# Two transformer stages in one kernel: the order of steps in the HGRN2 heads, and the weight low parts in four GpSimd instructions

## The reference, cut to what matters

```python
def hgrn2_mixer(h, w_in, lower_bound, norm_gain, w_o):
    q, f, i, g = jnp.split(h @ w_in, 4, axis=-1)
    q = jax.nn.silu(q)
    forget = lb + (1.0 - lb) * jax.nn.sigmoid(f)      # lb is 0 for the first layer of its kind
    log_f = jnp.log(forget)
    k = -jnp.expm1(log_f)
    # S_t = diag(f_t) S_{t-1} + k_t v_t^T ; o_t = S_t^T q_t, per head
    o = hgrn2_chunk_scan(heads(q), heads(k), heads(i), heads(log_f))
    o = rmsnorm(o, norm_gain) * jax.nn.sigmoid(g)
    return o @ w_o
```

## Time and profile before

| | us |
|---|---|
| median of 3 runs | 2027.22 (2027.17 to 2029.34) |
| the profiled execution | 2029.74 |
| its span | 2027.9 |

### The profile page before, as it was taken

How to read it: one execution, slowest core, us unless ns; L and a number is a source line. 1 busy time by engine, 2 the same in 40 slices (tenths; PEclk the granted TensorE clock), 3 DMA queues, 4 the chain that set the end, 5 groups by cost and what they waited for, 6 DMA issues and landing times.

```text
span 2027.9 us, 25756 instructions
## 1 busy us (share of the span) xinstructions
PE 1883.6 (93%) x8662; PEld 1469.3 (72%) x8662; DVE 1187.5 (59%) x1691; ACT 877.1 (43%) x1385; POOL 770.5 (38%) x402
## 2 busy tenths in 40 slices
PE   7999889999999999989899999998999987999988
PEld 5666568887888777878788887886776656776756
DVE  5667668614753677677577317724575556665561
ACT  6676634312433445544443213323554533554441
POOL 3222134444444555456344443443332213332212
PEclk9999999999999999999899999998999999999999
DMA  4212125433532211112145334422221212221212
GB/s 147 63 53 62 42 83 152 148 94 114 166 114 94 83 53 53 52 52 63 31 132 164 109 103 146 155 94 73 73 64 62 63 42 83 70 66 54 71 42 73
DMA packets 49223, 175.28 MB, mean 86 GB/s; under 512 B 5472, under 2 KB 5600, under 8 KB 49136
## 3 DMA queue, kind: packets, MB, share of 16 engines
q1 hardware_dynamic: 42224, 148.98, 23.7%
q10 hardware_dynamic: 6912, 25.17, 3.9%
HBM read 172.03 MB, written 2.10 MB: 86 GB/s over the span
## 4 chain that ended last, share of the span: by engine, by line
PE 38%; DVE 8%; ACT 4%; issue 4%; POOL 1%; ACTq 0%; DVEq 0%; POOLq 0%
PE ps_g L222 11%; PE ps_g L226 11%; PE ps_g L229 10%; DVE scr L1598 1%; DVE scr L431 1%; PE ps_o L1485 1%; PE ps_s L1424 1%; PE ps_zt L931 1%; DVE sml L1664 1%; PE ps_zt L1471 1%; DVE scr L293 1%; ACT scr L425 0%; POOL w_lo L210 0%; DVE scr L1624 0%; DVE a_lo L1632 0%
## 5 line engine op out<-in xcount | busy, mean ns | idle before, releaser
L210 POOL TENSOR_TENSOR w_lo<-raw,w_hi 128x1024 fp32r<-128x1024 f32 x274 | 670.6, 2448 | 1153.0 <-ACT w_hi L205 1153.0
L222 PE MATMUL ps_g<-h_hi,w_hi 128*128 128x512 f32 x1424 | 419.4, 423 | 40.2 <-DVE scr L1572 11.6
L205 ACT ACTIVATE w_hi<-raw 128x1024 fp32r<-128x1024 f32 x274 | 288.9, 1054 | 382.6 <-PE ps_g L229 376.7
L226 PE MATMUL ps_g<-h_lo,w_hi 128*128 128x512 f32 x1424 | 383.1, 399 | 0.2 <-DVE h_lo L255 0.2
L229 PE MATMUL ps_g<-h_hi,w_lo 128*128 128x512 f32 x1424 | 376.9, 394 | 0.0
L222 PEld LDWEIGHTS ps_g<-h_hi,w_hi 128*128 128x128 f32 x1424 | 259.8, 194 | 127.0 <-issue 63.5
L226 PEld LDWEIGHTS ps_g<-h_lo,w_hi 128*128 128x128 f32 x1424 | 275.0, 193 | 63.5 <-DVE h_lo L255 1.2
L229 PEld LDWEIGHTS ps_g<-h_hi,w_lo 128*128 128x128 f32 x1424 | 272.1, 191 | 58.7
L222 PE MATMUL ps_g<-a_hi,w_hi 128*128 128x512 f32 x768 | 205.2, 403 | 17.8 <-DVE a_lo L1632 7.5
L226 PE MATMUL ps_g<-a_lo,w_hi 128*128 128x512 f32 x768 | 197.2, 393 | 0.0
L229 PE MATMUL ps_g<-a_hi,w_lo 128*128 128x512 f32 x768 | 196.7, 392 | 0.0
(11 more groups left out here) (168 smaller groups left out, 2090.3 us busy)
## 6 DMA issues: line engine op xcount, KB each, us to landing
raw<-weights SPq DMA_DIRECT2D x274, 512.0 KB, 3.5
scr<-ada_weights ACTq DMA_DIRECT2D x48, 512.0 KB, 4.4
x<-x_tiles SPq DMA_DIRECT2D x8, 256.0 KB, 5.5
y<-x SPq DMA_DIRECT2D x8, 256.0 KB, 3.2
lvmask<-level_masks SPq DMA_DIRECT2D x1, 512.0 KB, 8.5
mats<-squares SPq DMA_DIRECT2D x1, 448.0 KB, 6.6
vecs<-vectors SPq DMA_DIRECT2D x1, 95.5 KB, 2.0
wgk<-gate_weights SPq DMA_DIRECT2D x1, 32.0 KB, 8.9
```

The source lines that it names most:

```text
L205: nc.scalar.activation(w_hi[:, t.rep % 2], raw[:, raw_slot(t)], ACT.Copy).then_inc(whi_ready, 1)
L210: nc.gpsimd.tensor_tensor(w_lo[:, t.rep % 2], raw[:, raw_slot(t)], w_hi[:, t.rep % 2].bitcast(F32), ALU.subtract).then_inc(wlo_ready, 1)
L222: nc.tensor.matmul(bank[:], w_hi[:, t.rep % 2, kk], rhs(k)[0], start=(first and n == 0), stop=False)
L226: nc.tensor.matmul(bank[:], w_hi[:, t.rep % 2, kk], rhs(k)[1], start=False, stop=False)
```

## The change

In `split_lo`, the one GpSimd subtraction over a tile (128 x 1024) becomes four over 128 x 256; the last one raises the semaphore. In the HGRN2 step, the gate of a part is taken in one piece on ACT, with its last Exp right behind the minimum; on VectorE the query's product follows at once, the front of part 3 of head `a` moves ahead of the scaled queries of level 1, and the front of part 0 of head `g` moves ahead of the selection of level 0 (`hg_sel_dve(dve, a, 1)`) and of the scaled queries of level 2; the decays between tiles come last, after level 6, on GpSimd, ACT and VectorE. The semaphore counts follow: level l is the (l+1)-th.

```diff
 def split_lo(pool, t):
     pool.wait_ge(whi_ready, t.of(1, 1))
-    nc.gpsimd.tensor_tensor(w_lo[:, t.rep % 2], raw[:, raw_slot(t)], w_hi[:, t.rep % 2].bitcast(F32),
-                            ALU.subtract).then_inc(wlo_ready, 1)
+    for i in range(0, KT, 2):
+        ks = slice(i, i + 2)
+        ins = nc.gpsimd.tensor_tensor(w_lo[:, t.rep % 2, ks], raw[:, raw_slot(t), ks],
+                                      w_hi[:, t.rep % 2, ks].bitcast(F32), ALU.subtract)
+    ins.then_inc(wlo_ready, 1)
...
 def hg_front_act(act, g, part):
...
     act.activation(ls_b, u_b[part % 2], ACT.Abs).then_inc(h_ls.abs_ready, 1)
-    h_ls.act(act, g.map(3, max(part - 1, 0)))
-
-def hg_last_act(act, g, part):
-    par = g.rep % 2
     if part == 0:
+        h_ls.act(act, g.map(3))
         act.wait_ge(hkf_ready, g.of(1, 1))
...
         act.activation(kk[par], kf_b, ACT.Exp).then_inc(hk_ready, 1)
     else:
+        n = g.map(3, part - 1)
         dst, done = (qq[par], hqe_ready) if part == 2 else (sg[par], hsg_ready)
-        act.wait_ge(h_ls.ready, g.of(3, part))
+        h_ls.act(act, n)
+        act.wait_ge(h_ls.ready, n.of(1, 1))
         act.activation(dst, dst, ACT.Exp).then_inc(done, 1)
...
 def hg_act(act, g, a, b):
...
-    if a: hg_last_act(act, a, 3)
     if g: hg_front_act(act, g, 0)
     if b: h_unit.act_rstd(act, b, hot_ready, b.v)
     if a: hg_e_act(act, a, 3)
-    if g: hg_last_act(act, g, 0)
...
-    if a: hg_e_act(act, a, 7)
     if a: hg_e_act(act, a, 4)
     if a: hg_e_act(act, a, 5)
     if g: split_hi(act, t + 4)
     if g: hg_front_act(act, g, 2)
     if a: hg_e_act(act, a, 6)
-    if g: hg_last_act(act, g, 2)
+    if a: hg_e_act(act, a, 7)
...
 def hg_front_dve(dve, g, part, stage=0):
...
     h_ls.dve_min(dve, n, bank, qq[par])
+    dve.wait_ge(hqe_ready, g.of(1, 1))
+    nc.vector.tensor_tensor(qq[par], qq[par], bank, ALU.mult).then_inc(hq_ready, 1)
...
 def hg_dve(dve, g, a, b):
     if a:
         hg_front_dve(dve, a, 3, 0)
         hg_qk_dve(dve, a, 0)
+        hg_front_dve(dve, a, 3, 1)
         hg_qk_dve(dve, a, 1)
     if g: hg_front_dve(dve, g, 0, 0)
+    if a: hg_sel_dve(dve, a, 0)
+    if g: hg_front_dve(dve, g, 0, 1)
     if a:
-        hg_front_dve(dve, a, 3, 1)
-        hg_sel_dve(dve, a, 0)
         hg_sel_dve(dve, a, 1)
         hg_qk_dve(dve, a, 2)
-    if g: hg_front_dve(dve, g, 0, 1)
...
         hg_qk_dve(dve, a, 4)
-        hg_qk_dve(dve, a, 7)
         hg_sel_dve(dve, a, 4)
...
         hg_sel_dve(dve, a, 6)
-    if g: hg_q_dve(dve, g)
-    if a: hg_sel_dve(dve, a, 7)
+        hg_qk_dve(dve, a, 7)
+        hg_sel_dve(dve, a, 7)
...
 def hg_pool(pool, g, a, b):
...
-    for i, l in enumerate([(2, 3, 7), (4, 5), (6,)]):
+    for i, l in enumerate([(2, 3), (4, 5), (6, 7)]):
```

More of the change, by code:

```diff
@@ L898, in build_program @@
         ORDER_HG = [NL - 1] + list(range(NL - 1))
[L899 to L905, removed]
         def hg_level_pe(pe, a, n):
@@ L914, in hg_level_pe @@
             else:
-                pe.wait_ge(hkp_ready, exp_n(a, l))
+                pe.wait_ge(hkp_ready, a.of(8, l + 1))
                 pe.wait_ge(hqk_ready, a.of(7, l + 1))
@@ L937, in part @@
                                         stop=True)
-            pe.wait_ge(hkp_ready, exp_n(a, 7))
+            pe.wait_ge(hkp_ready, a.of(8, 8))
             pe.wait_ge(hqr_ready, a.of(4, 4))
@@ L1008, in hg_e_act @@
                 act.wait_ge(hinter_ready, a.of(2))
-                act.wait_ge(hdk_ready, exp_n(a, 7))
+                act.wait_ge(hdk_ready, a.of(8, 8))
                 act.activation(kl_b[:, 0:SEQ - P], d_b[1][:, 0:SEQ - P], ACT.Exp, scale=-1.0).then_inc(hkp_ready, 1)
@@ L1017, in hg_e_act @@
             act.activation(blocks(e2_b[l % 2], n), d[:, :, n:2 * n], ACT.Exp).then_inc(he_ready, 1)
-            act.wait_ge(hdk_ready, exp_n(a, l))
+            act.wait_ge(hdk_ready, a.of(8, l + 1))
             act.wait_ge(hlev_ready, a.of(NL, l if l >= 2 else 0))
@@ L1023, in hg_front_act @@
         def hg_front_act(act, g, part):
+            t, par = g.map(4, T_HG), g.rep % 2
             act.wait_ge(hu_ready, g.of(4, part + 1))
@@ L1141, in hg_qk_dve @@
                                         ALU.mult).then_inc(hqr_ready, 1)
-                dve.wait_ge(hkp_ready, exp_n(a, 7))
+                dve.wait_ge(hkp_ready, a.of(8, 8))
                 nc.vector.tensor_scalar(kv_b[:, 0:P], kl_b[:, 0:P], eb_b[:, 2 * P - 1:2 * P], None,
@@ L1225, in hg_d_pool @@
             pool.wait_ge(hc_ready, a.of(1, 1))
-            pool.wait_ge(hkp_ready, exp_n(a, PREV_HG[l]) if l >= 2 else a.of(8))
+            pool.wait_ge(hkp_ready, a.of(8, max(l - 1, 0)))
             if l == 7:
```

## The result

The changed kernel takes 2002.5 us at the median (four runs, 1998.5 to 2002.6), the kernel before 2027.9 in the same comparison: ratio 0.9869 with a 95% interval of 0.9852 to 0.9886, so 25 us or 1.3% faster. The forecast was 2015, 12 us faster. The sign held, the time lies in the whole range of 1997 to 2036 but outside the forecast's own range of 2005 to 2022; the gain is twice what was summed.

A forecast was written before the change was run, and what follows sets the result against it. TensorE, busy 93% of the span, bounds the kernel, so only its idle or lower clock can be won. Part 1 (-7) and part 2 (-5) take 2027.2 to 2015 us; own range 2005 to 2022, whole range 1997 to 2036.

The forecast's parts named there:

- the second block's term of part 1: Second block: shorter holds of L1572 (2 us) and L1632 (2.8 us) by low parts, about 5 us won.
- part 1: Low parts in four GpSimd pieces of 128x256 instead of one instruction: -7 us, bounds 0 and -14.
- The clock: TensorE's granted clock, 0.95 in HGRN2: no term in the sum, only in part 1's bound, R1 and R3.
- the output projections: Starts of the two output projections: a low part's hold costs about 1 us each, 2 us won.
- Part 2: Former order of steps in HGRN2: waits per head from 3.5 to 2.8 us, -5 us; bounds -22 and +14.
- the prediction's own sign: HGRN2: part 2 is wrong if the pitch of L1229's successor isn't between 38.5 and 39.5 us a head.
- R1: Rival: HGRN2's chain escapes GpSimd, level 2 only 0.4 us late, half-speed stretches shrink; 1997 us, chance 0.15.
- R3: Rival, slower: HGRN2's wait at level 2 becomes the cost, with lower-clock stretches; 2036 to 2041, say 2038 us, chance 0.20.
- Part 1 in HGRN2: Pieces in HGRN2: no gain summed, as the gain is full only for single VectorE instructions.
- The rule of the conserved sum: A run of two-input VectorE instructions meets the pieces one after another, so the sum of waits stays as before.
- the cover: GpSimd's idle and zero wait of w_lo matmuls hide 0.1 us more per tile; without it, 27 us cost.
- R2: Rival: nothing measurable, 2027 us (2023 to 2031), chance 0.15; includes that four queued pieces hold VectorE as one.

The follow-up runs named there:

- the kernel with the decays in the middle: Kernel before with four pieces, gates in one piece and front ahead of level 2's queries, decays left between levels 3 and 4: 1988.1 us, ratio 0.9805.

## Why the prediction was right or wrong

The step that failed is the second block's term of part 1, which was sized at a third of what it brought; it is 10 of the 13 us that the forecast missed. The clock, which the forecast left at nothing, and the pieces in HGRN2 brought about 3 us each, and of the 2 us forecast for the output projections at most 1 came.

**Part 1 in the second block: right place, a third of the size.** I had -2.4 us a layer from two kinds of wait, about 5 us; with the pieces there alone the kernel is 15 us faster, and its layers lost 7.3 and 8.5 us (7.4 and 8.7 in the changed kernel). Little of it is clock: in the changed kernel the idle of the two layers fell by 6.3 and 5.9 us. I had taken L1572 for the instruction that is held. In sum over both layers it isn't: its form with two SBUF inputs went from 14.6 to 18.5 us, and its median over 16 instructions from 0.69 to 1.22 us: more of them now meet a piece, though a short one. What was held is the minimum ahead of it (L431, now L434), and `a_lo` (L1632, now L1621), as these groups of VectorE over the two layers show, first before, then changed (busy us, mean ns of one, idle before):

```profile
L431 DVE SCALAR_TENSOR_TENSOR scr<-scr 128x512 f32<-128x512 f32 x20 | 27.8, 1391 | 6.5 <-ACT scr L427 6.5
L1632 DVE TENSOR_TENSOR a_lo<-scr,a_hi 128x512 fp32r<-128x512 f32 x16 | 25.3, 1582 | 1.4 <-ACT a_hi L1547 1.4
L1572 DVE SCALAR_TENSOR_TENSOR scr<-scr 128x512 f32<-128x512 f32 x16 | 14.6, 912 | 1.6
```

```profile
L1561 DVE SCALAR_TENSOR_TENSOR scr<-scr 128x512 f32<-128x512 f32 x16 | 18.5, 1158 | 0.0
L1621 DVE TENSOR_TENSOR a_lo<-scr,a_hi 128x512 fp32r<-128x512 f32 x16 | 15.7, 982 | 1.4 <-ACT a_hi L1536 1.4
L434 DVE SCALAR_TENSOR_TENSOR scr<-scr 128x512 f32<-128x512 f32 x20 | 14.4, 721 | 5.9 <-ACT scr L430 5.9
```

Wait by wait, in the first layer: L1617's two of 0.7 us went as predicted (-1.4). The wait at 1458.27 fell from 3.73 to 1.57 us, 2.2 and not 1.0: I took one hold off and found ACT's L427 next, but the minima of the three tiles ahead (at 1435.70, 1442.15 and 1448.59) had been held as well, 1.71, 1.71 and 1.70 us, where they now take 0.74, 0.74 and 0.75. The sum over L1572 fell by 1.7 us (its two other waits grew by 0.4 together), a chain that I hadn't looked at, ACT's L1563 behind VectorE, by 1.4, and small ones by about 1.8. The longest L1572 went from 2.46 to 1.23 us and the longest L1632 from 2.90 to 1.23, near the 1.0 forecast.

**Part 2, its sum of waits: right, its pitch: not.** The idle per head was to fall from 3.5 to 2.8 us, 5 us in all; the idle of the stretch fell by 4.9, and with the order alone the span less the clock's cost is 5 us shorter. The wait at level 2 was taken as 2.3 us and is 1.89; the inter part was taken as 0.5 and is 0.50; the waits of 1.57 and 2.87 us are gone. One make-up was wrong: I let three pieces of a low part stand between VectorE's instructions. Only the last piece touches the front, and the 1.0 us that the scans lose is level 4's subtraction (I called it level 3's). By the prediction's own sign part 2 is wrong all the same: the pitch was to be 38.5 to 39.5 us a head and is 37.7. Idle accounts for 0.7 of the 2.0 us and 17.1 us less at 1.2 GHz over seven heads for 1.2 more; that is the clock.

**The clock: left at nothing in the forecast.** A gain of clock stood only in part 1's bound and in R1, a loss in R3, and the sum of the forecast had neither. In the profiled pair the stretch of HGRN2 has 8.5 us of it, the larger part of its 10.0 us less busy time. Over all executions the estimate above leaves 3 to 4 us of it to the change, and 7 of the 12 us to the order alone. The granted clock of 0.95 in the earlier trace rows was in front of me: 5% of 312 us is 16 us of loss, in the stage in which I moved the waits. In the table of stretches less idle goes with less time at 1.2 GHz, roughly and not in every pair of rows.

**Part 1 in HGRN2: nearly nothing, but not for my reason.** I argued that a run of VectorE instructions meets the pieces one after another, so that nothing is won. In the new order the pieces shorten the stretch by 3.6 us (320.4 to 316.8), 0.9 of it idle, so for the forecast itself zero was close. In the order of before they brought 28.8 us in this stage (331.7 to 302.9), 16.6 of it idle; that profiled execution was 7 us faster than its kernel's median. VectorE's busy time in the stretch fell from 227.6 to 201.4 us there, and from 205.9 to 181.7 in the new order: 24 to 26 us less hold in both. The rule of the conserved sum is refuted as a rule. It looks true at level 2 of the new order only because the low part isn't what is met there. One piece is 0.74 us, so a single instruction is held that long and not 2.4; in the order of before the chains behind level 3 and the decays, as I read it, had slack for the short hold and not for the long one. There the 1.57 us wait is at most 0.3, and what is left is this, at the turn:

```profile
743.85 0.66 PE L405 MATMUL ps_zt<-mats,scr 128*128 128x128 f32 x4 [0.62 <-DVE scr L1101]
```

**The starts of the output projections (-2): 1 us at most.** The one behind HGRN2, with its MLP, takes 403.2 us instead of 402.3; all that stands ahead of HGRN2, with the other one in it, takes 667.7 instead of 668.8.

**A piece: 0.74 us, not 0.63.** Four take 3.0 us where 2.40 did one. The Trainium skill (GPSIMD Engine Reference, section 3.1) gave 3.1 by its cycles and my estimate of the dispatch, closer than my row. By that rule the forecast would have been 3 to 4 us higher, and the result is 13 lower: the cover held in every tile of the changed kernel (TensorE's idle before L232 is 0.0 us), so that the longer low part cost TensorE no wait for `w_lo`. Where it fails is in the kernel with the decays in the middle, 1.70 us a head.

**The rivals.** R2's rule, that queued pieces hold VectorE as one, is refuted by the timeline of the changed kernel: a minimum, which reads two tensors, begins and ends while four pieces run.

```profile
1430.77 3.46 POOL L212 TENSOR_TENSOR w_lo<-raw,w_hi 128x256 fp32r<-128x256 f32 x4 [2.35 <-ACT w_hi L205]
...
1432.01 0.75 DVE L434 SCALAR_TENSOR_TENSOR scr<-scr 128x512 f32<-128x512 f32 x1
```

The Trainium skill (SBUF — State Buffer, Who interferes with whom) left this open; here VectorE gets in between queued GpSimd instructions. R1's time, 1997, is nearer than the forecast's, but not for its reason: level 2 was late by what the forecast said. R3's mechanism, the wait at level 2, stands and costs 18 to 21 us against the same kernel without it (2002 to 1984.8 or 1981.8); it doesn't show against the kernel before, which had worse waits.

What stays open: why the lower clock follows a wait of 1.89 us in some heads and not in others, and why the clock's cost differs in stages that an edit leaves alone. The second block, with the same code, takes 609.0 us in the changed kernel's profiled execution and 602.6 in that of the pieces alone, so part of the 18 us between the two isn't in HGRN2 at all.

## What to carry to other kernels

Read which instruction of the other engine really lies on top of the held one before cutting anything: here cutting the low parts helped wherever they were on top, and did nothing where it was another subtraction. Sum the held time of every VectorE line in a stage; the longest instruction in a timeline (here L1572) needn't be the one that is held most. Two changes that take away the same waits don't add up, and the second can cost; test each alone, and move what TensorE waits for next ahead of a long chain. When the granted clock is below 1.00 in a stage, price the waits there with the clock on both sides, a gain as well as a loss, and read its size from several executions, not from one trace.

## What the runs showed of the hardware

GpSimd's two-input subtraction with 1024, 512, 256 and 128 values per partition takes 2.40, 1.30, 0.74 and 0.46 us at the median, so by the medians each further instruction adds about 0.19 us (4 x 0.742 = 2.97, 2.97 - 2.40 = 0.57, over three). These are the rows of one, two and eight:

```profile
L210 POOL TENSOR_TENSOR w_lo<-raw,w_hi x274: 2337/2400/3075, 6.5 to 2015.1; 128x1024 fp32r<-128x1024 f32 x137
```

```profile
L212 POOL TENSOR_TENSOR w_lo<-raw,w_hi x548: 1260/1295/2262, 5.9 to 1992.3; 128x512 fp32r<-128x512 f32 x183
```

```profile
L212 POOL TENSOR_TENSOR w_lo<-raw,w_hi x2192: 446/462/1529, 6.3 to 1998.3; 128x128 fp32r<-128x128 f32 x200
```

I had not expected that a wait on GpSimd's queue, put there on purpose, could save 18 us: GpSimd silent for 2.7 us cost nothing, and four scans took 1.36 us instead of 2.39. By the estimate from the clocks only about 3 of these 18 us are waits, and 14 are time that the lower clock no longer costs, some of it in other stages.
